# Reloading stored products through ScalarE's DMA queue, with later low parts and respread modulation steps, in a one-layer trunk kernel

## The reference

```python
mod = jax.nn.silu(c) @ w_ada[l] + b_ada[l]
shift1, scale1, gate1, shift2, scale2, gate2 = jnp.split(mod[:, None, :], 6, axis=-1)
h = modulate(rmsnorm(x, norm_mix_g[l]), shift1, scale1)
proj = h @ w_in[l]
...            # attention heads and mLSTM heads, concatenated
x = x + gate1 * (mixed @ w_out[l])
h2 = modulate(rmsnorm(x, norm_mlp_g[l]), shift2, scale2)
y = jnp.square(jax.nn.relu(h2 @ w_ff1[l])) @ w_ff2[l]     # 2048 -> 8192 -> 2048
x = x + gate2 * y
```

## Time and profile before

| | |
|---|---|
| median of three runs | 2308.79 us |
| profiled execution, its own time | 2306.21 us |
| its span | 2304.3 us |
| granted TensorE clock, mean | 0.986 |
| PE busy | 2198.8 us (95%) |
| VectorE (DVE) busy | 1777.0 us (77%) |
| ScalarE (ACT) busy | 1025.9 us (45%) |
| feed-forward groups 0 to 30 in the span | 991.4 to 2261.4 us |

### The profile page before, as it was taken

The page is one execution under the profiler, slowest core; times in us unless marked ns, Lnnn a source line. Parts: engine busy times, 40 slices in busy tenths (PEclk is TensorE's granted clock), DMA queues, the critical chain, the costliest instruction groups (busy, mean ns, idle before and its releaser), DMA issues.

```text
span 2304.3 us, 31643 instructions
## 1 busy us (share of the span) xinstructions
PE 2198.8 (95%) x12452; PEld 1929.1 (84%) x12452; DVE 1777.0 (77%) x1945; ACT 1025.9 (45%) x1371; POOL 325.7 (14%) x183
## 2 busy tenths in 40 slices
PE   6999999999999999999999999999889999999999
PEld 6888888888877878889999999999777777877777
DVE  5877877766545875688898888988877788888786
ACT  5435453543355222555555555565433333333331
POOL 2004434343421444300000000000000000000000
PEclk9999999999999999999999999999999999999999
DMA  9965445544656697246575575654855756645541
GB/s 347 328 218 206 158 158 183 177 170 165 229 196 231 228 333 237 82 139 227 203 265 192 209 258 194 229 218 164 313 199 201 251 181 220 242 150 216 201 146 74
DMA packets 261329, 480.16 MB, mean 208 GB/s; under 512 B 18874, under 2 KB 105404, under 8 KB 258368
## 3 DMA queue, kind: packets, MB, share of 16 engines
q1 hardware_dynamic: 237136, 397.94, 50.7%
q10 hardware_dynamic: 24048, 80.23, 8.8%
HBM read 389.48 MB, written 88.63 MB: 207 GB/s over the span
## 4 chain that ended last, share of the span: by engine, by line
PE 53%; DVE 23%; DMA 9%; issue 9%; ACT 5%; POOL 1%; SPq 1%; DVEq 0%; ACTq 0%; POOLq 0%
PE ps L978 10%; PE ps L980 9%; PE ps L979 9%; DMA st<-in_w_ff 7%; DVE wlo L2878 6%; PE ps L1519 4%; PE ps L1521 4%; PE ps L1520 4%; ACT whi L2035 3%; PE ps L1475 3%; PE ps L1476 3%; PE ps L1477 3%; DVE tlo L2860 2%; DVE yacc L2960 2%; DVE acc L2974 1%
## 5 line engine op out<-in xcount | busy, mean ns | idle before, releaser
L1475 PE MATMUL ps<-hc,whi 128*128 128x256 f32 x1680 | 479.5, 285 | 20.2 <-DVE cb L2946 14.5
L1476 PE MATMUL ps<-hc,whi 128*128 128x256 f32 x1680 | 478.1, 285 | 0.0
L1477 PE MATMUL ps<-hc,wlo 128*128 128x256 f32 x1680 | 477.9, 284 | 0.0
L1519 PE MATMUL ps<-whi,ab 128*128 128x512 f32 x840 | 332.4, 396 | 33.9 <-DVE yacc L2960 22.8
L500 POOL TENSOR_TENSOR wlo<-wraw,whi 128x1024 fp32r<-128x1024 f32 (+3 forms) x116 | 290.1, 2512 | 479.5 <-ACT whi L495 439.5
L1475 PEld LDWEIGHTS ps<-hc,whi 128*128 128x128 f32 x1680 | 325.1, 194 | 23.0 <-issue 16.1
L2035 ACT ACTIVATE whi<-st 128x1024 fp32r<-128x1024 f32 x180 | 190.5, 1058 | 313.4 <-DMA st<-in_w_ff 140.1
L1521 PE MATMUL ps<-whi,ab 128*128 128x512 f32 x840 | 328.8, 391 | 0.0
L1520 PE MATMUL ps<-wlo,ab 128*128 128x512 f32 x840 | 328.8, 391 | 0.0
L1477 PEld LDWEIGHTS ps<-hc,wlo 128*128 128x128 f32 x1680 | 325.2, 194 | 0.0
L1476 PEld LDWEIGHTS ps<-hc,whi 128*128 128x128 f32 x1680 | 325.1, 194 | 0.0
(11 more groups left out here) (361 smaller groups left out, 4026.4 us busy)
## 6 DMA issues: line engine op xcount, KB each, us to landing
wraw<-in_w_ff SPq DMA_DIRECT2D x128, 512.0 KB, 6.3
st<-in_w_ff SPq DMA_DIRECT2D x120, 512.0 KB, 10.2
araw<-in_w_ada SPq DMA_DIRECT2D x112, 512.0 KB, 6.6
a_d<-ring ACTq DMA_DIRECT2D x109, 512.0 KB, 5.1
ab<-a_d SPq DMA_DIRECT2D x105, 512.0 KB, 8.3
wraw<-in_w_in SPq DMA_DIRECT2D x72, 512.0 KB, 6.1
arawx<-in_w_ada SPq DMA_DIRECT2D x48, 512.0 KB, 4.7
wraw<-in_w_out SPq DMA_DIRECT2D x32, 512.0 KB, 7.8
```

The costliest lines, as they stand in the source:

```text
L1475: pe.matmul(dst, w[0][:, c], hi, start=new, stop=False, skip_group_check=True)
L1476: pe.matmul(dst, w[0][:, c], lo, start=False, stop=False, skip_group_check=True)
L1477: ins = pe.matmul(dst, w[1][:, c], hi, start=False, stop=t == 3, skip_group_check=True)
L1519: pe.matmul(dst, hi, w[0], start=new, stop=False, skip_group_check=True)
```

## The change

Four things change in the code.

1. The reloads of `ab` are issued by ScalarE instead of SyncE (`comb_load`, `comb_loads`, `stored_wait`), each behind the same wait for its block, just after the high part of a step; ScalarE has waited for that block already there. SyncE issues only weight pieces, and what loads are rare.
2. The low part of q = 1's blocks is made one step later (`step_low`): one step instead of two ahead of TensorE.
3. Form 3 is made one step later in the second product too (`back_of`).
4. The gate's steps are two in groups 1 to 5 and 8 to 12 and three in groups 6, 7, 13 and 14 (`gate2_at`). `ada_sum` stands in groups 7 and 14, before step 11, and `ada_cols` at step 13 of the same groups.

```diff
 def back_of(t, g):
     if blocks_of(g) == 1:
         return {3: 2, 2: 1}.get(t, 0)
-    return int(t == 3 and g < GROUPS_A)
+    return int(t == 3)
...
 def gate2_at(g, j):
-    s = 3 * (g - 1) + j
-    if g < 7:
-        return s if s < 16 else G2_STEPS
-    return s - 2
+    half, turn = (g - 1) // 7, (g - 1) % 7
+    s = 2 * turn + max(0, turn - 5) + j
+    return 16 * half + s if j < 2 + (turn >= 5) and half < 2 else G2_STEPS
...
             gate2_load(gate2_at(g + 1, 0))
-            if g == GROUPS_A - 1:
-                stored_wait(PRODUCTS)
-                for q, free in ((0, 0), (1, 0), (2, 2), (3, 2), (6, 1), (5, 5), (4, 5)):
-                    if q == 5:
-                        piece_load(g + 1, 3)
-                    sp.wait_ge(blk_done, FF_AT["W", g, free, 1] + 1)
-                    comb_load(g + 1, q)
-            else:
-                piece_load(g + 1, 3)
+            piece_load(g + 1, 3)
         for r in range(4):
             piece_load(GROUPS_A + 1, r)
         for g in range(GROUPS_A, LAST):
-            turn = (g - GROUPS_A) % 2 == 1
-            for q in SEQ:
-                if 3 <= TURN[q] < 7 and g > GROUPS_A:
-                    piece_load(g + 1, (1, 0, 2, 3)[TURN[q] - 3])
-                if turn or g == GROUPS_A:
-                    sp.wait_ge(blk_done, FF_AT["W", g, q, blocks_of(g) - 1] + 1)
-                if g == GROUPS_A:
...
-                elif turn:
-                    comb_load(g + 1, q)
+            for r in (1, 0, 2, 3):
+                if g > GROUPS_A:
+                    piece_load(g + 1, r)
...
-                if key[2:] == (5, 0) and g in (6, 12):
-                    ada_sum(10 if g == 6 else 11, acc2[:, 0:2, :], 7)
+                if key[2:] == (5, 1) and g in (7, 14):
+                    ada_sum(9 + g // 7, acc2[:, 0:2, :], 7)
...
+        def comb_load(g, q, after, parts=(0, 1)):
+            act.wait_ge(blk_done, FF_AT["W", after[0], after[1], blocks_of(after[0]) - 1] + 1)
+            for i, c in enumerate(chunks_of(g)):
+                if i in parts:
+                    act.dma_start(ab[q][:, :, 2 * i:2 * i + 2, :].rearrange("p a k n -> p a (k n)").bitcast(F),
+                                  a_d[:, c, q, :, :]).then_inc(ab_in[q], 16)
+
+        def comb_loads(g, s):
+            if s == 0 and g > GROUPS_A and (g <= GROUPS_A + 2 or (g - GROUPS_A) % 2 == 0):
+                after, q = g - 1, SEQ[6]
+            elif g <= GROUPS_A + 1 and 1 <= s < 7:
+                after, q = g, SEQ[s - 1]
+            elif (g - GROUPS_A) % 2 == 1 and g != LAST and s % 2 == 0 and s >= 2:
+                after, q = g, SEQ[s // 2 - 1]
+            else:
+                return
...
+                if g == GROUPS_A - 1:
+                    if s == 2:
+                        stored_wait(PRODUCTS)
+                    for q, after in {2: ((0, 0), (1, 0)), 6: ((2, 2), (3, 2)), 8: ((6, 1),),
+                                     12: ((5, 5), (4, 5))}.get(s, ()):
+                        comb_load(g + 1, q, (g, after))
...
         def step_low(p):
-            if p + 2 < len(FF_ORDER):
-                weight_low(FF_ORDER[p + 2])
+            late, key = [FF_ORDER[p + d] if p + d < len(FF_ORDER) else ("", 0, 0, 0) for d in (1, 2)]
+            if late[0] == "W" and late[2] == 1:
+                weight_low(late)
+            if key[0] and not (key[0] == "W" and key[2] == 1):
+                weight_low(key)
...
-                if g in (7, 13) and s == 1:
-                    m = M_G2 + 8 * (g == 13)
-                    ada_cols(10 if g == 7 else 11, 7, m, m + 4)
+                if g in (7, 14) and s == 13:
+                    m = M_G2 + 8 * (g == 14)
+                    ada_cols(9 + g // 7, 7, m, m + 4)
```

More of the change, by code:

```diff
@@ L794, in gate2_load @@
                              .rearrange("p (w n) -> p w n", w=2)).then_inc(ada_loaded[4], 16)
[L796 to L802, removed]
         def stored_wait(count):
@@ L2093, in a_store, with stored_wait @@
             act.dma_start(a_d[:, c, q, :, :], ring[:, slot, :, :]).then_inc(a_stored[slot], 16)
+        def stored_wait(count):
+            for i in range(4):
+                act.wait_ge(a_stored[i], STORED_0 + 16 * ((count - i + 3) // 4))
+        def comb_load(g, q, after, parts=(0, 1)):
[13 more added lines that the diff above has]
+                return
+            if (g, s) == (GROUPS_A, 1):
+                stored_wait(PRODUCTS * 3)
+            elif (g, s) == (GROUPS_A + 3, 2):
+                stored_wait(PRODUCTS * (CHUNKS - 1) + 4)
+            if after <= GROUPS_A + 1:
+                comb_load(GROUPS_A + 2, q, (after, q), (1,) if after == GROUPS_A else (0,))
+            else:
+                comb_load(after + 1, q, (after, q))
         def relu_square(src, tile, count):
@@ L2175, in _ @@
         p0 = GB + 14 * GROUPS_A
+        place = [(g, s) for g in range(GROUPS_A, GROUPS) for s in range(len(group_order(g)))]
         for p in range(p0, len(FF_ORDER)):
             step_hi(p)
+            if p - p0 < len(place):
+                comb_loads(*place[p - p0])
             if p == p0:
```

## The result

The changed kernel took 2249.41 us in the median of four runs (2247.34 to 2255.52), against 2307.99 us for the kernel before in the same comparison: 0.9755 of it, 95% interval 0.9713 to 0.9798. Run again beside other kernels it took 2249.79 us, 0.9759 (0.9742 to 0.9775). The forecast was 2258 us. The profiled execution took 2249.78 us, its span is 2248.0 us.

A forecast was written before the change was run, and what follows sets the result against it. The prediction took TensorE as the bound, held up some 27 times by a late VectorE. Savings of 16 + 12 + 20 = 48 us off 2306.2 us gave 2258 us; the forecast's own range was 2246 to 2270, the whole range 2242 to 2284.

The forecast's parts named there:

- A: First product, groups 1 to 14: later low part and fewer gate steps save 16 us, bounds 8 and 18.
- B: Groups 15 and 16: taking the reloads off SyncE saves 12 of 18.9 us, bounds 3 and 17.
- C: Groups 17 to 29: four causes together save 20 of 23.4 us, bounds 8 and 23.4.
- iv of C: Groups 17 to 29: VectorE's two gaps behind form 1 go, so steps 4 to 7 take 10.3 us, not 12.5.
- i of C: Groups 17 to 29: both reloads of q = 2 start before the contested pieces, so the piece comes 2.7 us earlier.
- (ii): Groups 17 to 29: form 3 is wanted one operation and one step later, some 1.1 to 2.7 us.
- (iii): Groups 17 to 29: the next group's first low part no longer stands behind form 3, so the starting wait goes.
- Costs on ScalarE: ScalarE's idle time covers issuing 98 and a few more reloads: cost nothing, bounds 0 and 4 us.
- 1.6 that I had named as the limit: Sign of the rival that ScalarE becomes late: issues over 1.6 us each; 2337 us, chance 0.04.
- wait for `ada_cols` ahead of group 15: Rival: a late last piece makes TensorE wait about 4 us before group 15; B is 8, 2262 us, chance 0.03.
- bandwidth rival: Reloads and pieces: full DMA engines, not queue order, make pieces late; B is 3, C some 11, 2276 us, chance 0.15.
- the gap: Sign that the forecast is right: no idle VectorE between form 1 and its low part, 1.12 us idle before.

The follow-up runs named there:

- late reloads: The changed kernel with the last four reloads of a reload group put off into the next group: 2245.50 us, 0.9752 of the kernel before.
- swapped order: The changed kernel with reloads back on SyncE's queue, the reload of q = 2 ahead of the first piece, first two pieces together behind it: 2244.31 us, one run.

## Why the prediction was right, point by point

The total was right, 2258 us against 2249.4, and the range held it, but the causes were right only in part. The terms as sizes: A was 16 us and is 586.9 - 568.1 = 18.8; B was 12 and is 57.3 - 46.7 = 10.6; C was 20 and is 523.8 - 502.4 = 21.4. Some 5.5 us came where I had forecast nothing: 3.2 ahead of group 0, in unchanged code, 2.0 in group 0, whose low parts also moved, and 0.3 from group 30 on.

That B and C came out so near is in part luck. B was put down to the reloads alone, and C in the first place to pieces that land sooner. But without moving the reloads the other parts give 13.6 us of B and 22.4 of C, more than the changed kernel has; the reloads alone give 8.5 and 10.6. The causes overlap, and I had added them as if they did not. C's upper bound was also too low: with the late reloads groups 17 to 29 are 28.7 us shorter than before, and the bound was 23.4.

- **Which engine makes TensorE wait, and at which steps**: right. Most waits did cost their idle time and some 0.17 us more: the nine waits for `cb` were priced at 16.0 us of A's 18.8. Of the other 2.8 us, 1.8 were in group 5, which took 45.2 us before, 4.9 more than a clean group, with a wait of 2.9: its granted clock was 0.96 where all its neighbours had 1.00. I had priced the lower clock in groups 15 and 16 and overlooked it here:

```profile
1210.40:1255.60 45.20, 42.28 (x339) 41.93 (x338) 38.34 (x40) 23.94 (x32) 0.00 (x0) 0.96 0.64 226
```

- **The gaps behind form 1 (A, and iv of C)**: right as a mechanism and much undervalued. I gave this part and the gate steps term A together, and C to four causes. Alone it gives 18.9 us in groups 1 to 14 and 20.5 in 17 to 29. The step that failed in sizing is the sum in C: it made the piece's lateness the main thing, and a wait of up to 4.7 us for it does little harm when VectorE has the slack (six waits of PE, 6.2 us in all, are left).
- **Fewer gate steps (A)**: not needed. Alone they shorten the nine groups by 15.6 us, but beside the later low part they are worth nothing. The longest wait, 2.9 us, was priced against 2.25 + 1.28 us of slack; the later low part alone was enough in all nine. And "moved, not changed: nothing" for `ada_sum` holds only beside the later low part; alone, it took back all that the steps gave.
- **Reloads off SyncE (B, and i of C)**: right alone (8.5 us of B, 10.6 of C), nothing on top of the rest. Point (i), that the piece would land 2.7 us sooner, came true with the reloads alone (2.5 us). In the changed kernel it landed 1.7 us sooner, and just as soon without the reloads' move: what the earlier issue gave, the longer way took back (14.2 us against 11.5), since the reloads now share the engines with the pieces instead of standing in front. What brought the pieces forward there is that VectorE, being less late, was done with the buffers 1.5 us earlier.
- **Form 3 later (ii)**: right. With form 3 at its old step VectorE is ready for it 30.9 us after the start of the reload groups, in the changed kernel 32.5 us; the 1.6 us are within the 1.1 to 2.7 forecast. Little of it reaches TensorE, 0.8 to 2.5 us in groups 17 to 29.
- **The low part ahead of form 3 (iii)**: the waits at the start of a group are gone, but the cause is not shown to be this one. They are gone too with the low part alone, and with form 3 put back to its old step.
- **Costs on ScalarE**: right. 105 reloads, 0.37 us each in the median, 1.32 at most, under the 1.6 that I had named as the limit (1.59 in the second profile). The wait for `ada_cols` ahead of group 15 did not come in the changed kernel; in the two with the new gate steps and the reloads on SyncE it was 1.7 and 1.8 us.
- **The rivals**: the bandwidth rival was right on the transfers of the changed kernel (the same landing with and without the move), not on those with the reloads alone, and wrong on the time. It took for granted that late pieces must reach TensorE.

Of the signs named, the waits for `cb` (none left), the gap and groups 15 and 16 with their clock came as said (46.7 us for 45); waits before form 3 are 15.5 us, just over the 15 named; groups 19, 21 and on took 38.5 to 40.2 us, mean 39.3, and not 38.7: that is the late landing of the pieces, which the late reloads and the swapped order made earlier.

Group 16 is shorter by 3 us or more with the reloads in SyncE's queue (22.8 us, against 25.9 and 27.5). The traces say where: the second `wraw` piece of group 17, for which TensorE in the end waits in the changed kernel, landed 17.8 us after the start of the group there (9.0 us under way) and 13.1 us in SyncE's queue alone (4.7 us under way). TensorE's long wait is 2.3 us in place of 3.8, and the clock stays at 1.00 instead of 0.93. Not settled is how much of this is the sharing of the engines, and how much the order and the earlier issue, since the two kernels differ in all of them.

## What to carry to other kernels

When an in-order engine stands still for a result that it has itself just set going, move that result's use one operation back before anything else: 2.25 us of slack per group gave 1.9% alone, the reloads' own queue 0.7%. A transfer on another queue did not get out of the way of the first one here; it shared the engines with it, and it was the order in which things are wanted, or a stretch with room, that made the first one land sooner. Parts of a change should be tried alone and left out one at a time: here two of four, the reloads' queue and the gate steps, were worth nothing that could be measured beside the others, and one of those looked like 0.7% by itself. And a part that moves work (`ada_sum`) can add a wait of its own that another part hides.

## What the runs showed of the hardware

- Two queues with 512 KB transfers under way divided the DMA engines 55.9% to 42.7%, and the median time to landing of the four `st` pieces of group 20 rose from 11.5 us (everything in one queue) to 14.2 us. With the other pieces in the queue but no reload beside them it was 7.3 us, and with the reloads in the same queue in another order 9.8 us.
- The issue of a transfer on ScalarE's queue took 0.37 us in the median over its 105 reloads, though two of SyncE's had taken 3.04 us with a longer row of transfers under way.
- In group 15 the granted clock rose from 0.87 to 1.00 when the 4.6 us wait before step 2 was gone; in group 16, which kept one wait of 3.8 us, from 0.89 to 0.93. Shorter waits went with a lower clock too: 0.96 in group 5 before, with a wait of 2.9 us, and 0.93 in groups 7 and 14 with the gate steps alone, with waits of 2.2 us ahead of `ada_sum`. A wait of 2.3 us in group 16 of the kernel with all but the reloads left it at 1.00. Some waits of TensorE here thus cost more than their length, others only their length.
